# Between the stages: a row of factors spread by transposes, the first chunk's high part made on VectorE, the second chunk added on GpSimd

## What is computed

```
x += 1/2 * post_norm(SwiGLU_1(pre_norm(x)))        # first FFN,  D_FF = 5632
h  = pre_norm(x);  p = h @ w_in                    # input projection, 6152 columns
mix = [mLSTM heads(p), conformer conv(p)] @ w_out  # 4 heads x 256, and 1024 conv channels
x += post_norm(mix)
x += 1/2 * post_norm(SwiGLU_2(pre_norm(x)))        # second FFN

rmsnorm(x, g) = x * rsqrt(mean(x*x) + 1e-6) * g    # over the 2048 features of a token
```

## Time and profile before

| | us |
|---|---|
| median of 3 runs | 2174.95 (2174.79 to 2175.0) |
| the profiled execution | 2175.0 |
| its span, first to last instruction | 2173.3 |
| PE busy | 2157.3, 99% of the span |
| DVE busy | 994.0, 46% |
| ACT busy | 901.7, 41% |
| POOL busy | 960.1, 44% |
| share of the chain that ended last: PE, DVE, ACT | 96%, 2%, 1% |
| DMA | 371.39 MB, mean 171 GB/s |

### The profile page before, as it was taken

How to read it: one execution, slowest core, us unless ns; L and a number is a source line. 1 busy time by engine, 2 the same in 40 slices (tenths; PEclk the granted TensorE clock), 3 DMA queues, 4 the chain that set the end, 5 groups by cost and what they waited for, 6 DMA issues and landing times.

```text
span 2173.3 us, 41900 instructions
## 1 busy us (share of the span) xinstructions
PE 2157.3 (99%) x16332; PEld 2147.2 (99%) x16332; DVE 994.0 (46%) x1402; ACT 901.7 (41%) x1167; POOL 960.1 (44%) x557
## 2 busy tenths in 40 slices
PE   9999999999999999999999999999999999999998
PEld 9999999999999999999999999999999999999997
DVE  6543332224343224978768737633332223333323
ACT  6434333333433335634345536433343333333343
POOL 1444443344444444566656331444443334444454
PEclk9999999999999999999999999999999999999999
DMA  6554554444455544555656543545455454545453
GB/s 241 165 166 162 166 168 168 164 165 165 163 165 163 174 159 144 205 185 205 220 179 213 192 159 136 178 160 172 163 167 168 162 169 160 171 161 171 161 169 112
DMA packets 101333, 371.39 MB, mean 171 GB/s; under 512 B 11360, under 2 KB 14048, under 8 KB 100224
## 3 DMA queue, kind: packets, MB, share of 16 engines
q1 hardware_dynamic: 96912, 349.64, 47.7%
q10 hardware_dynamic: 4208, 20.47, 2.6%
q0 software_dynamic: 128, 0.07, 0.0%
HBM read 357.06 MB, written 13.07 MB: 170 GB/s over the span
## 4 chain that ended last, share of the span: by engine, by line
PE 96%; DVE 2%; ACT 1%; DMA 0%; issue 0%; POOL 0%; SPq 0%; POOLq 0%; ACTq 0%; DVEq 0%
PE bank L433 30%; PE bank L431 30%; PE bank L432 30%; PE bank L746 1%; PE bank L748 1%; PE bank L747 1%; DMA raw<-stream 0%; DVE wlo L1180 0%; PE bank L681 0%; PE bank L685 0%; ACT whi L816 0%; PE bank L640 0%; PE bank L622 0%; DVE y L1263 0%; PE bank L496 0%
## 5 line engine op out<-in xcount | busy, mean ns | idle before, releaser
L1673 POOL TENSOR_TENSOR wlo<-raw,whi 128x1024 fp32r<-128x1024 f32 x332 | 798.8, 2408 | 884.7 <-ACT whi L816 768.8
L431 PE MATMUL bank<-xh,whi 128*128 128x288 f32 x3585 | 1064.4, 297 | 2.3 <-DVE wlo L1180 1.2
L432 PE MATMUL bank<-xl,whi 128*128 128x288 f32 x3585 | 1059.2, 295 | 0.0
L433 PE MATMUL bank<-xh,wlo 128*128 128x288 f32 x3585 | 1057.9, 295 | 0.0
L816 ACT ACTIVATE whi<-raw 128x1024 fp32r<-128x1024 f32 x657 | 692.7, 1056 | 610.8 <-PE bank L433 580.4
L1180 DVE TENSOR_TENSOR wlo<-raw,whi 128x1024 fp32r<-128x1024 f32 x325 | 470.6, 1449 | 775.2 <-ACT whi L816 773.9
L431 PEld LDWEIGHTS bank<-xh,whi 128*128 128x128 f32 x3585 | 676.1, 189 | 5.1 <-DVE xl L1195 1.6
L433 PEld LDWEIGHTS bank<-xh,wlo 128*128 128x128 f32 x3585 | 675.0, 188 | 0.0
L432 PEld LDWEIGHTS bank<-xl,whi 128*128 128x128 f32 x3585 | 674.0, 188 | 0.4
L433 PE MATMUL bank<-hh,wlo 128*128 128x288 f32 x1408 | 417.4, 296 | 0.0
L431 PE MATMUL bank<-hh,whi 128*128 128x288 f32 x1408 | 416.1, 296 | 0.0
(11 more groups left out here) (246 smaller groups left out, 1082.2 us busy)
## 6 DMA issues: line engine op xcount, KB each, us to landing
raw<-stream SPq DMA_DIRECT2D x657, 512.0 KB, 3.4
C<-c_in ACTq DMA_DIRECT2D x4, 2048.0 KB, 8.7
cs_out<-C ACTq DMA_DIRECT2D x4, 2048.0 KB, 7.6
conv_out<-upad ACTq DMA_DIRECT2D x4, 302.0 KB, 6.3
x_res<-x_in SPq DMA_DIRECT2D x2, 576.0 KB, 8.7
y_out<-x_res SPq DMA_DIRECT2D x4, 288.0 KB, 2.7
upad<-conv_in ACTq DMA_DIRECT2D x4, 272.0 KB, 3.2
cp_out<-cpr ACTq DMA_DIRECT2D x4, 256.0 KB, 9.0
```

What stands on the lines that cost most here:

```text
L431: pe.matmul(out, wh, mov_hi[:, k, :], start=first, stop=False)
L432: pe.matmul(out, wh, mov_lo[:, k, :], start=False, stop=False)
L433: return pe.matmul(out, wl, mov_hi[:, k, :], start=False, stop=last)
L1673: pool.tensor_tensor(wlo[:, g % SLOTS, :], raw[:, g % SLOTS, :], whi[:, g % SLOTS, :].bitcast(F32), ALU.subtract).then_inc(lo_ready[g % SL ...
```

## The change

Line numbers of the changed kernel are 2 to 43 higher than those of before. It does the following.

- `post_norm` spreads the factors by `pe.transpose` of the broadcast column, three of 128 x 128 for a row, and at A and B does so into two banks, 4 and 5.
- `early_operands` on ACT, ahead of the load of the root's table: `x[:, 0, :]` times the next stage's gain into `scr`, and `y[:, 1, :]` times the post gain in place.
- Chunk 0: DVE multiplies y by gain and row into bank 6, makes `xh[:, 0, :]` from it and `scr` itself, adds x into the bank, and makes `xl[:, 0, :]` from the bank. ACT later copies the bank to x and squares it.
- Chunk 1: ACT copies the row of bank 5 to `rpost`; POOL multiplies `y[:, 1, :]` by it and adds x (`second_chunk`); ACT and DVE make the high and low part as before.
- The low part of piece 3 goes from POOL to DVE, ahead of chunk 5. PE's first multiplication also waits for `rpost`, since its first tile takes bank 5.

```diff
-NEXT_LOW = {4: 7, 5: 9, 6: 11, 7: 13, 8: 15, 9: 16, 10: 16, 11: 16}
+NEXT_LOW = {3: 5, 4: 7, 5: 9, 6: 11, 7: 13, 8: 15, 9: 16, 10: 16, 11: 16}
...
-        for begin, n in ((0, 0), (GATE_P, 4), (FFN2_P, 4)):
+        for begin, n in ((0, 0), (GATE_P, 3), (FFN2_P, 3)):
...
                 pe.wait_ge(x_hi, x_from + 1)
+                if x_from:
+                    pe.wait_ge(rpost_ready, x_from // XC)
...
-                    for c, (lo, n) in enumerate(((0, P), (P, P), (2 * P, NS))):
-                        mm = pe.matmul(bank[b][:, lo:lo + n], nfac[:, c:c + 1].broadcast_to([P, P]),
-                                       ident[:, P - n:P], start=True, stop=True)
+                    for c, lo in enumerate(BLOCKS):
+                        mm = pe.transpose(bank[b][:, lo:lo + P], nfac[:, c:c + 1].broadcast_to([P, P]), ident[:, :])
                     mm.then_inc(norm_row, 1)
...
-            post_norm(0, (4,))
+            post_norm(0, (4, 5))
...
+            def early_operands(pre, post):
+
+                act.activation(scr[:, 0, :], x[:, 0, :], ACT.Copy, scale=gain(pre, 0)).then_inc(old_first, 1)
+                act.activation(y[:, 1, :], y[:, 1, :], ACT.Copy, scale=gain(post, 1)).then_inc(y_second, 1)
+
+            def x_operands(g, pre, stage, splits):
+
+                n_new, n_x = (XC - 2) * stage, XC * (stage + 1)
+                act.wait_ge(norm_row, 2 * stage + 2)
+                act.activation(rpost[:, :], bank[5][:, 0:TOK], ACT.Copy).then_inc(rpost_ready, 1)
+                for c in range(1, XC):
...
+                    if c == 1:
+                        act.wait_ge(x_second, stage + 1)
+                        act.wait_ge(x_hi, n_x + 1)
+                    else:
+                        act.wait_ge(x_new, n_new + c - 1)
                     act.activation(xh[:, c, :], x[:, c, :], ACT.Copy, scale=gain(pre, c)).then_inc(x_hi, 1)
                     act.activation(y[:, c, :], x[:, c, :], ACT.Square).then_inc(xsq_ready, 1)
+                    if c == 1:
+                        act.wait_ge(x_ready, n_x + 1)
+                        act.activation(x[:, 0, :], bank[6][:, 0:TOK], ACT.Copy)
+                        act.activation(y[:, 0, :], bank[6][:, 0:TOK], ACT.Square).then_inc(xsq_ready, 1)
...
+                                if norm_at == 1:
+                                    early_operands("g_mix_pre", "g_ffn1_post")
                                 load_table(norm_at, ACT.Sqrt)
...
+            early_operands("g_ffn2_pre", "g_mix_post")
             load_table(3, ACT.Sqrt)
...
+            def residual(g, stage, T, post, pre):
+
+                n_x, n_t, n_new = XC * (stage + 1), XC * stage, (XC - 2) * stage
+                dve.wait_ge(norm_row, 2 * stage + 1)
+                t = bank[6][:, 0:TOK]
+                dve.scalar_tensor_tensor(out=t, in0=y[:, 0, :], scalar=gain(post, 0), in1=bank[4][:, 0:TOK],
+                                         op0=ALU.mult, op1=ALU.mult).then_inc(t_ready, 1)
+                dve.wait_ge(t_ready, n_t + 1)
+                dve.wait_ge(old_first, stage + 1)
+                dve.scalar_tensor_tensor(out=xh[:, 0, :], in0=t, scalar=gain(pre, 0), in1=scr[:, 0, :],
+                                         op0=ALU.mult, op1=ALU.add).then_inc(x_hi, 1)
+                dve.wait_ge(x_hi, n_x + 1)
+                dve.tensor_tensor(t, t, x[:, 0, :], ALU.add).then_inc(t_ready, 1)
+                dve.wait_ge(t_ready, n_t + 2)
+                dve.scalar_tensor_tensor(out=xl[:, 0, :], in0=t, scalar=gain(pre, 0), in1=xh[:, 0, :].bitcast(F32),
+                                         op0=ALU.mult, op1=ALU.subtract).then_inc(x_ready, 1)
+                for m, c in enumerate(range(2, XC)):
+                    for p in NEXT_LOW:
+                        if NEXT_LOW[p] == c:
+                            split_lo(g + p)
+                    t = bank[7 - m % 2][:, 0:TOK]
+                    if m == 1:
+                        dve.wait_ge(xsq_ready, n_x + 2)
...
+            def second_chunk(stage):
+
+                pool.wait_ge(rpost_ready, stage + 1)
+                pool.wait_ge(y_second, stage + 1)
+                pool.tensor_tensor(y[:, 1, :], y[:, 1, :], rpost[:, :], ALU.mult).then_inc(pool_t, 1)
+                pool.wait_ge(pool_t, stage + 1)
+                pool.tensor_tensor(x[:, 1, :], y[:, 1, :], x[:, 1, :], ALU.add).then_inc(x_second, 1)
+
             ffn(0, 0, 0, 0, 0)
-            split_lo(GATE_P + 3)
+            second_chunk(0)
...
-            split_lo(FFN2_P + 3)
+            second_chunk(1)
```

More of the change, by code:

```diff
@@ L327, in hybrid_layer_kernel @@
         out0_done = sem("out0_done")
+        old_first, y_second, x_second = sem("old_first"), sem("y_second"), sem("x_second")
         nn_ready = sem("nn_ready")
@@ L798, in _ @@
                     out_half(OUT_T + q, OUT_P + 4 + q, True, i)
-            post_norm(1, (4,))
+            post_norm(1, (4, 5))
             keep_warm(6)
@@ L832, in post_root @@
                                bias=eps[:, int(factor > 1):int(factor > 1) + 1]).then_inc(norm_sd, 1)
-            def x_operands(g, pre, n_new, splits):
-                for c in range(XC):
+            def early_operands(pre, post):
[6 more added lines that the diff above has]
+                for c in range(1, XC):
                     for p in splits:
@@ L1159, in _ @@
             split_hi(FFN2_P + 3)
-            x_operands(FFN2_P, "g_ffn2_pre", XC, NEXT_SPLITS)
+            x_operands(FFN2_P, "g_ffn2_pre", 1, NEXT_SPLITS)
             act.wait_ge(cs_stored, 16 * H)
@@ L1165, in _ @@
             post_root(5, 4.0)
-            act.wait_ge(norm_row, 4)
+            act.wait_ge(norm_row, 6)
             act.activation(rpost[:, :], bank[5][:, 0:TOK], ACT.Copy).then_inc(rpost_ready, 1)
@@ L1221, in first_operands @@
                 dve.wait_ge(vec_landed, 16)
[L1223 to L1241, removed]
+            def residual(g, stage, T, post, pre):
[20 more added lines that the diff above has]
+                        dve.wait_ge(xsq_ready, n_x + 2)
+                    if m > 1:
+                        dve.wait_ge(x_new, n_new + m - 1)
+                    if c == XC - 1:
+                        dve.wait_ge(tile_evicted, T)
+                    dve.scalar_tensor_tensor(out=t, in0=y[:, c, :], scalar=gain(post, c), in1=bank[4][:, 0:TOK],
+                                             op0=ALU.mult, op1=ALU.mult).then_inc(t_ready, 1)
+                    dve.wait_ge(t_ready, n_t + m + 3)
+                    dve.tensor_tensor(x[:, c, :], t, x[:, c, :], ALU.add).then_inc(x_new, 1)
+                    x_lo(pre, c - 1, n_x)
+                x_lo(pre, XC - 1, n_x)
@@ L1246, in last_residual @@
             def last_residual():
-                dve.wait_ge(norm_row, 3)
+                dve.wait_ge(norm_row, 5)
                 dve.wait_ge(y_scaled, LAST_GROUPS[-1][1])
@@ L1373, in _ @@
             post_factor(1)
-            residual(GATE_P, 0, GATE_T, "g_ffn1_post", "g_mix_pre", XC, 0)
+            residual(GATE_P, 0, GATE_T, "g_ffn1_post", "g_mix_pre")
             square_tree(2 * XC)
@@ L1655, in _ @@
             post_factor(3)
-            residual(FFN2_P, 1, FFN2_T, "g_mix_post", "g_ffn2_pre", 2 * XC, XC)
+            residual(FFN2_P, 1, FFN2_T, "g_mix_post", "g_ffn2_pre")
             square_tree(3 * XC)
@@ L1858, in _ @@
                     add_sq(1, p - 4, 4, XC // 4 - 1)
-            split_lo(FFN2_P + 3)
+            second_chunk(1)
             ffn(FFN2_P, FFN2_T, sum(FF_HALVES), 2, 2)
-            pool.wait_ge(rpost_ready, 1)
+            pool.wait_ge(rpost_ready, 3)
             pool.wait_ge(y_scaled, XC)
@@ L1866, in _ @@
                 pool.tensor_tensor(y[:, a:b, :], y[:, a:b, :], row, ALU.mult).then_inc(pool_t, 1)
-                pool.wait_ge(pool_t, n + 1)
+                pool.wait_ge(pool_t, n + 3)
                 pool.tensor_tensor(x[:, a:b, :], y[:, a:b, :], x[:, a:b, :], ALU.add).then_inc(y_pool, 1)
```

1 line of the change is left out of this document (removed).

## The result

| us | before | after |
|---|---|---|
| median (22 runs each) | 2175.09 (2174.47 to 2175.76) | 2178.09 (2177.25 to 2178.84) |
| span of the profiled execution | 2173.3 | 2176.3 |

The ratio is 1.0014, 95% interval 1.0008 to 1.0020: slower by 3.0 us, less than the 0.2% that I counted as a difference, but outside the scatter. The forecast was 2178.0.

The account below looks back on a forecast made before the run. VectorE's chain to its tree of squares was taken to set PE's waits: A 1.36, B 2.00 and end -0.3 gave +3.06 on 2175.0, so 2178.0 us, range 2175.3 to 2179.5.

Parts of the forecast that it names:

- The bound: At A and B, VectorE's chain to its tree of squares sets when PE passes line 491, not PE's start.
- Early operands: Two more ACT instructions ahead of the table load make T (start of line 511) 0.24 later at A, 0.88 at B.
- From T to chunk 3: From the start of line 511 (T), VectorE's chunk 3 starts at T+4.70, before T+4.71, waiting for ACT's square from bank 6.
- Piece 3: Low part moved onto VectorE's chain costs 1.13 there; counted from T, the tree ends 1.12 later at A and B.
- The size: Whole kernel: A 1.36, B 2.00 and end -0.3 make +3.06 on 2175.0, so 2178.0; chance 0.79.
- PE's waits: Before line 491, PE waits about 1 us longer for the tree at both boundaries; piece 9's low part may stop it briefly.
- The end: At the kernel's end, transposes make both rows sooner: -0.3, between -0.6 and 0.
- The gain at the head: Rival at A and B: piece fits VectorE's idle time, PE keeps 0.45 each; 2174.9, or 2173.8 with early operands hidden; chance 0.11.
- POOL was not late: Rival at A and B: chunk 1 on POOL comes late and delays chunk 3 and the tree, for instance 2181.2; chance 0.06.
- clock: Rival: clock falls to 1.2 GHz while PE waits at B; 2.5 at each boundary, 1 covered, some 2181; chance 0.04.
- The rule of the port: VectorE beside POOL's chunk 1: blocking could cost up to 0.81; nothing counted, as chunks 0 and 2 use a bank.
- The transposes: Making the rows: 0.10 per transpose taken, both rows by T+0.95; 275 ns each in series would give near T+1.7.

Follow-up runs that it names:

- before_p3: The kernel before with piece 3's low part moved from POOL to VectorE ahead of chunk 5 at both boundaries; 2176.68 us (1.0009).
- before_early: The kernel before with two spare copies with a gain, read by nobody, on ACT ahead of the two table loads; 2176.28 us (1.0007).
- early_moved: The changed kernel with the two early ACT operands moved to idle stretches of ACT at A and B; 2176.60 us (1.0008).
- after_look: The changed kernel run and profiled once more, unaltered; 2177.94 us (1.0014).
- bank_free: The changed kernel with VectorE's chunk 3 in bank 7, so it no longer waits for ACT's square out of bank 6; 2176.82 us (1.0010).
- before_transposes: The kernel before with the row of factors spread by three transposes, into bank 4 only at A and B; 2174.42 us (0.9999).
- p3_on_pool: The changed kernel with piece 3's low part back on POOL, behind chunk 1; 2177.49 us (1.0013).
- sums_later: The changed kernel with PE's sum of squares and its wait for the tree four blocks later, at B only; 2177.15 us (1.0010).

## Why the prediction was right, point by point

- **The bound.** VectorE's chain sets the pace and not PE's start. Right: in before_p3 a piece of 1.13 on VectorE alone delays the run by 0.9 to 1.0 at each boundary, and in the changed kernel PE starts 0.51 earlier and is 1.20 later at line 494.
- **Early operands.** +0.24 and +0.88 were predicted; before_early shows +0.20 and +0.93, and early_moved takes them away again.
- **From T to chunk 3.** T+4.70 was predicted; it was T+4.60 at A (853.56 - 848.96), and T+4.66 at B in after_look. The wait for ACT's square was 0.41 for my 0.5, and bank_free shows that it was real and worth 0.5. PE's first product came at T+1.96 for my T+2.2, which changed nothing.
- **Piece 3.** 1.12 was predicted for each chain; it was +1.05 and +1.20, and +1.04 and +1.02 without the fall of the clock. The piece itself took 1.14; the 0.1 less is chunk 3, at T+4.60 and not T+4.70. That POOL's piece no longer held VectorE's first low part (0.2) is no further term: before, the hold stands inside the T+4.71, and after, the wait for ACT's square sets chunk 3.
- **The size.** That +3.06 met +3.1 in the profile is in part luck. The first profile holds about 0.25 from a fall of the clock, for which the sum had nothing; after_look, without it, has +2.8, since each boundary came out 0.1 cheaper than forecast.
- **PE's waits.** I expected about 1 us more before line 494. It was 0.84 and 0.59 more; the rest at A lay before the low part of piece 8, which VectorE makes ahead of chunk 15 (876.26 to 877.49 at A). I had looked for it at piece 9. The sum is not touched, as the text had put both into one account.
- **The end.** -0.3 was predicted and came in all kernels with transposes.
- **The rivals.** The gain at the head did not stay: before_transposes shows that not even before would have kept it. POOL was not late: its pair took 852.03 - 850.35 = 1.68, predicted 1.69. The *clock* did fall, and the step that failed there is the price. I let about 5 us at the lower level cost 2.5, of which only 1 found cover. It was 3.4 us; PE's first product at B came at T+3.27 instead of T+1.96. In after_look PE waits 0.78 and 1.02 for VectorE at B, in the first profile only 0.78 at line 494: these waits took up 1.0. What is left is 0.2 in the profiles, and perhaps up to 0.9 by the executions' mean clock (above). So the rival's price of 3 us for both boundaries was far too high. The fall itself is not rare: if a mean clock of 0.997 marks it, it came in 12 of 22 executions.
- **The rule of the port.** The Trainium skill (SBUF — State Buffer, Terms) has VectorE and GpSimd share a port pair that one holds for a whole instruction. The trace agrees with it in the low parts of the earlier trace rows and of the experiments. I counted nothing for the new order, and rightly: VectorE's instructions beside POOL's pair lasted 0.47 to 0.52. But I read the earlier trace rows as a curiosity of B (at A the same low part had 0.69). It was the key to the transposes' lost 0.3 and to p3_on_pool, which came out 1.1 above the 2176.4 of giving the piece back free of charge.
- **The transposes.** By my estimate from the 275 ns of the Trainium skill (TensorE: Matmul & The Clock Gate, Part 4) the second row would have been ready near T+1.7. ACT's copy of it started at 849.86, T+0.90. The trace agrees with the figure as the length of one transpose (0.27 each), but not as the distance from one to the next: six take 0.70 up to the next matmul's start.

Seen from the end, the change buys 0.1 up to chunk 3 of a chain that then has 1.14 more to do, and pays 1.1 ahead of it. No version here beats the kernel before by what can be measured; the nearest is before_transposes, 0.3 us.

## What to carry to other kernels

When one engine is 99% busy, find which engine's chain ends its few waits and measure from that chain's start to its end; an earlier start of the busy engine is worth nothing if it waits for the same chain later. Count what leaves and what enters that chain: here one chunk's two instructions left, a high part and a piece entered. And before moving work to GpSimd, look at the instructions of VectorE beside it: here those with all tensors in SBUF ended only behind GpSimd's.

## What the hardware showed that I had not expected

- VectorE's instruction of 0.51 took up to 2.05 when it was issued behind the start of a POOL instruction of 2.37, and it ended 0.32 after POOL's each time (851.98, 854.35 and 854.53 for 851.66, 854.03 and 854.21). VectorE's instructions with a bank among their operands kept their 0.46 to 0.52 in the same time. The same can be read all over the trace of before, ahead of any experiment: 178 of VectorE's own low parts of pieces start while POOL makes one, and each ends 1.08 to 1.13 after POOL's, so that some take up to 3.20 for the 1.22 of an undisturbed one. The first of them here:

```profile
65.20 2.40 POOL L1673 TENSOR_TENSOR wlo<-raw,whi 128x1024 fp32r<-128x1024 f32 x1 [2.07 <-ACT whi L816]
...
66.11 2.57 DVE L1180 TENSOR_TENSOR wlo<-raw,whi 128x1024 fp32r<-128x1024 f32 x1 [1.44 <-ACT whi L816]
```

- About 0.9 us of idle PE ahead of a short burst was followed by a granted clock of 0.50 for about 3.4 us in all in three kernels (after, bank_free, sums_later) and by 1.00 in three others with the same idle time (before_early, p3_on_pool, after_look); after and after_look are the same program. Without the idle time it fell at B in none of the eight other profiles. What decides between the cases stays open.
